# Five small constant loads issued behind the three weight blocks of the first projection, and a semaphore of its own for the rotation table

## The reference, cut to what matters

```python
proj = x @ w_in                      # 512x1024 @ 1024x1536
q, k, v = split(proj)                # 16 query heads, 4 key heads, 4 value heads
q = partial_rope(q, pos); k = partial_rope(k, pos)    # table of cos and sin: rope
...
probs = softmax(concat([scores, sink_col]))[..., :-1]  # swa_sinks
...
logits = (h2 @ w_router) + b_router                    # the router, after attention
...
f_logit = proj[..., 3 * hd_all:] + b_f                 # layer 1, forget gate: fox_b_f, last 16 columns of fox_w_in
```

## Time and profile before

| | us |
|---|---|
| median of three timed runs | 936.52 (936.02 to 937.94) |
| the profiled execution | 930.61 |
| its span, first to last instruction | 928.8 |
| around the span | 1.8 |
| PE busy | 890.1 (96%) |
| DVE busy | 537.9 (58%) |
| ACT busy | 379.0 (41%) |
| POOL busy | 119.8 (13%) |
| mean clock granted to TensorE | 0.994 of full |

### The profile page before, as it was taken

One profiled execution on the slowest core, in us unless ns is written; L12 is line 12 of the kernel. 1 busy time (PEld: TensorE's weight loads), 2 busy tenths in 40 slices (PEclk: granted clock), 3 DMA queues, 4 the chain that ended last, 5 costly groups with the idle time before them and its releaser, 6 DMA issues.

```text
span 928.8 us, 12393 instructions
## 1 busy us (share of the span) xinstructions
PE 890.1 (96%) x4460; PEld 611.9 (66%) x4460; DVE 537.9 (58%) x1110; ACT 379.0 (41%) x763; POOL 119.8 (13%) x137
## 2 busy tenths in 40 slices
PE   8899999999999999989999999999999999999985
PEld 7787777885665665537778886565786566665632
DVE  3543886457777677475323223777456866677617
ACT  3321887001555555331132224777301355555400
POOL 2000232102110000030000000232211210010021
PEclk9999999999999999999999999999999999999998
DMA  9941000018999998655053222111105999999335
GB/s 315 348 174 74 40 2 1 23 46 328 344 382 389 377 384 330 227 205 181 0 181 138 91 91 91 47 48 46 52 40 226 314 386 387 384 389 402 101 107 199
DMA packets 49701, 183.14 MB, mean 197 GB/s; under 512 B 6560, under 2 KB 6560, under 8 KB 41456
## 3 DMA queue, kind: packets, MB, share of 16 engines
q1 hardware_dynamic: 35712, 132.34, 37.8%
q0 software_dynamic: 9200, 33.33, 11.0%
q10 hardware_dynamic: 4736, 16.78, 4.7%
HBM read 159.60 MB, written 22.84 MB: 196 GB/s over the span
## 4 chain that ended last, share of the span: by engine, by line
PE 87%; DVE 5%; DMA 3%; issue 1%; SPq 1%; ACT 1%; POOL 0%; DVEq 0%; POOLq 0%; ACTq 0%
PE bank L557 17%; PE bank L558 17%; PE bank L559 17%; PE bank L843 12%; PE bank L674 4%; PE bank L655 4%; PE bank L812 3%; PE bank L699 2%; PE bank L499 2%; PE bank L718 2%; PE bank L531 2%; PE bank L760 2%; PE bank L513 1%; DMA ring<-in_swa_w_in 1%; DMA arena<-ys,pos 1%
## 5 line engine op out<-in xcount | busy, mean ns | idle before, releaser
L1406 DVE TENSOR_TENSOR gu_low<-ring,gu_high 128x1024 fp32r<-128x1024 f32 x128 | 151.2, 1222 | 53.3 <-ACT gu_high L1063 53.3
L1063 ACT CAST gu_high<-ring 128x1024 fp32r<-128x1024 f32 x128 | 127.7, 1048 | 18.5 <-DVE arena L1542 18.5
L843 PE MATMUL bank<-ring,arena 128*96 128x512 f32 x256 | 115.8, 595 | 2.9 <-DVE arena L1532 1.8
L557 PE MATMUL bank<-gu_high,rows_high 128*96 128x512 f32 x256 | 112.4, 439 | 2.5 <-DVE rows_low L1526 2.5
L558 PE MATMUL bank<-gu_low,rows_high 128*96 128x512 f32 x256 | 101.0, 395 | 0.0
L559 PE MATMUL bank<-gu_high,rows_low 128*96 128x512 f32 x256 | 100.5, 393 | 0.0
L843 PEld LDWEIGHTS bank<-ring,arena 128*96 128x96 f32 x256 | 39.7, 165 | 55.3 <-issue 54.5
L995 ACT ACTIVATE arena<-arena,nmax 128x256 f32<-128x256 f32 (+3 forms) x128 | 66.8, 523 | 20.9 <-DVE nmax L1299 10.8
L557 PE MATMUL bank<-high,x_high 128*128 128x512 f32 x160 | 64.9, 406 | 6.2 <-DVE xlow L1209 3.5
L447 POOL TENSOR_TENSOR low<-ring,high 128x512 fp32r<-128x512 f32 x32 | 40.6, 1270 | 227.7 <-ACT high L1023 227.7
L558 PE MATMUL bank<-low,x_high 128*128 128x512 f32 x160 | 63.9, 400 | 0.0
(11 more groups left out here) (227 smaller groups left out, 1499.4 us busy)
## 6 DMA issues: line engine op xcount, KB each, us to landing
ring<-in_w_gate SPq DMA_DIRECT2D x32, 1024.0 KB, 13.6
ring<-in_w_up SPq DMA_DIRECT2D x32, 1024.0 KB, 16.0
ring<-in_w_down SPq DMA_DIRECT2D x32, 1024.0 KB, 16.3
ys<-arena ACTq DMA_DIRECT2D x32, 384.0 KB, 7.6
ring<-in_fox_w_in SPq DMA_DIRECT2D x6, 2048.0 KB, 9.4
ring<-in_swa_w_in SPq DMA_DIRECT2D x2, 2048.0 KB, 13.4
ring<-in_swa_w_o SPq DMA_DIRECT2D x2, 2048.0 KB, 17.6
xd<-xres ACTq DMA_DIRECT2D x8, 512.0 KB, 2.6
```

What stands on the lines that cost most here:

```text
L557: eng.matmul(out, ah, wh, start=(c == 0), stop=False)
L843: mm = eng.matmul(bank[5 + half][0:CAP, :], hT[:, b, c, :], w[:, c, half * BLK:(half + 1) * BLK], start=(c == 0), stop=(c == FC - 1))
L1063: eng.copy(gu_high[u % 2][:, :, part, :], slot_gate_up(use)[:, :, part, :]).then_inc(S("gu_high"), 1)
L1406: eng.tensor_tensor(gu_low[use % RING][:, :, part, :], slot_gate_up(use)[:, :, part, :], gu_high[u % 2][:, :, part, :], ALU.subtract).then ...
```

## The change

The five small loads that nobody reads in the projection (`sink`, `wr`, `br`, `bf`, `wf`) are issued behind block 2. The rotation table stays where it was and gets the semaphore `rope_in`. Tiles 2 and 3 of x follow it directly. DVE waits for `rope_in` at its old place, and for the other five (`const_in`, now 80) at the start of the last group, k = 11, where it now negates the sinks. PE waits for 80 instead of 96 ahead of the router.

```diff
                     if l == 0 and j == 0:
                         load_x(1)
-                        eng.dma_start(cs[:, :, :, :], rope.rearrange("(t p) a n -> p t a n", p=P)).then_inc(S("const_in"), 16)
+                        eng.dma_start(cs[:, :, :, :], rope.rearrange("(t p) a n -> p t a n", p=P)).then_inc(S("rope_in"), 16)
+                        load_x(2)
+                        load_x(3)
+                    if l == 0 and j == IN_BLOCKS[0] - 1:
                         eng.dma_start(sink[:, :], swa_sinks[0].partition_broadcast(P)).then_inc(S("const_in"), 16)
                         eng.dma_start(wr[:, :, :], w_router.rearrange("(c p) n -> p c n", p=P)).then_inc(S("const_in"), 16)
                         eng.dma_start(br[:, :], b_router.partition_broadcast(P)).then_inc(S("const_in"), 16)
                         eng.dma_start(bf[:, :], fox_b_f.rearrange("a h -> h a")).then_inc(S("const_in"), 16)
                         eng.dma_start(wf[:, :, :], fox_w_in[0][:, 3 * D:3 * D + NH].rearrange("(c p) n -> p c n", p=P)).then_inc(S("const_in"), 16)
-                        load_x(2)
-                        load_x(3)
...
                     if t == 0:
-                        eng.wait_ge(S("const_in"), 96)
+                        eng.wait_ge(S("const_in"), 80)
...
-            eng.wait_ge(S("const_in"), 96)
-            link(eng.tensor_scalar(sink[:, :], sink[:, :], -1.0, None, ALU.mult))
+            eng.wait_ge(S("rope_in"), 16)
...
                     for k in range(GROUPS[0]):
                         j, t = k // NT, k % NT
+                        if k == GROUPS[0] - 1:
+                            eng.wait_ge(S("const_in"), 80)
+                            link(eng.tensor_scalar(sink[:, :], sink[:, :], -1.0, None, ALU.mult))
                         if k + 1 < NT:
                             x_low(k + 1)
```

## The result

| | before | changed |
|---|---|---|
| median of seven runs, us | 936.02 (932.88 to 937.94) | 928.77 (926.73 to 931.24) |
| ratio of the runs | | 0.9932, interval 0.9916 to 0.9949 |
| profiled execution, its span, us | 930.61, 928.8 | 928.77, 927.0 |

By the ratio the change is worth 6.4 us (4.8 to 7.9), not 3.9; a second measurement (experiment 12) gives 5.3 us (3.5 to 7.1). The two profiled spans differ by 1.8 us only, and why that is no measure of the change is one of the things to be learned here.

The account below looks back on a forecast made before the run. PE was taken to bound the kernel, with a 3.52 us stall at group 2 behind block 1's load. An earlier landing (2.3 us) plus the clock (1.56) gave 3.9 us, 936.5 to 932.6 us, range 931.0 to 935.0.

Parts of the forecast that it names:

- The bound: PE stands 3.52 us at group 2, since ACT waits for block 1; PE starts 2.72 us after block 1 lands.
- the landing: Block 1's load lands at 20.9 instead of 23.26, 2.3 us earlier, leaving a stall of 1.2 us at group 2.
- Rival A: PE's stall at group 2 goes wholly, block 1 landing by 19.74: gain 5.1 us, time 931.4; chance 0.12.
- the trough: DMA at 10 to 14 us: 164 instead of 398 GB/s, from small pieces and SP's hold, costing 2.35 us.
- The clock: PE's clock no longer falls in the 4.42 us behind the group 2 stall: 1.56 us come back.
- the new semaphore: DVE waits for the table alone at its old place: nothing gained, nothing lost.
- the wait at group 11: DVE's added wait for the five loads and the negation fit in 4.50 us of idle time: cost 0.
- POOL: Gets block 2 earlier and starts clearing `ys` some 2 us before 29.41: cost 0.
- SP's queue: Issue of block 1 or 2 takes several us, but a full queue holds SP, not the transfers: cost 0.
- B: The clock behind group 2's stall falls all the same, only 2.3 us won: 934.2; chance 0.15.
- C: SP's stop moves from `br` to block 1, which lands near 23, no earlier: 936.5; chance 0.07.
- D: Queue not served in order, so block 0 and groups 0 and 1 come late: 5.8 us slower, 942.4; chance 0.04.

Follow-up runs that it names:

- experiment 12: The changed kernel measured again as it is: 929.84 us, ratio 0.9943 to before.
- Experiment 1: Kernel before, loads untouched; ACT and DVE make the next block's weight pieces behind the next tile of x instead of ahead of it: 928.13 us, ratio 0.9937.
- experiment 3: Changed kernel, but only `wr` and `wf` moved behind block 2; `sink`, `br`, `bf` stay in front: 933.27 us, ratio 0.9988.
- experiment 4: Changed kernel, but only `sink`, `br`, `bf` moved behind block 2; `wr` and `wf` stay in front: 935.0 us, ratio 1.0002.
- experiment 5: Changed kernel with the load of `sink` alone back between the table and tile 2: 932.27 us in one run.
- experiment 10: Changed kernel with the load of `wr` alone back between the table and tile 2: 934.87 us in one run.
- experiment 11: Changed kernel with `sink` alone in front, the same program repeated and timed: 932.55 us, ratio 0.9976.
- experiment 9: Changed kernel plus a probe load ahead of tile 2, 128 pieces of 64 bytes from different rows of x, read by nobody: 930.01 us in one run.
- Experiment 2: Kernel before with only the change's semaphores, all loads in the old order: 933.45 us, ratio 0.9991.

## Why the prediction was wrong, point by point

*The bound was right.* The wait, its cause on ACT, the 2.72 us from landing to start: the six stalls measured later follow from it. With `wr` and `wf` gone, 22.03 + 2.7 = 24.7, and PE started at 24.72; in the other five PE started 2.69 to 2.70 us behind ACT's first piece as well. Experiment 1 shows the cause by itself.

*The step that failed is the landing.* "Sum 2.35 + 0.37 - 0.42 = 2.3 us. Block 1 lands at 23.26 - 2.3 = 20.9." It moved by 3.9 us in the profiled execution, and by 3.1 in experiment 12 (23.26 to 20.15). What the sum left out can in part be read from the trace that I had. Up to block 1's landing before, and in the changed kernel (length, clock, DMA share, GB/s):

```profile
0.00:23.26 23.26, 1.00 0.91 315
```

```profile
0.00:19.36 19.36, 1.00 0.93 345
```

23.26 us at 315 GB/s are 7.33 MB; x, block 0 and block 1 (2.1 MB each) with the table and the small loads (0.21), all that lies in the queue up to the last piece of block 1, are 6.50. So 0.8 MB from behind block 1 had passed before block 1 was whole. With the change it is 6.68 MB against 6.36, 0.3 MB. The 0.5 MB between them, at 390 GB/s, are 1.3 us. And the table, for which I kept 0.42 us, cost next to nothing (391 GB/s with it in the stretch). 2.35 + 0.37 + 1.3 is 4.0. The same reckoning on the other traces gives 0.5 MB (experiment 12) and 0.6 (probe or `bf` in front) where block 1 lands at 20.1 to 20.5, and 0.7 to 1.1 in experiments 3, 4, 5, 10 and 11, where it lands at 22.0 to 23.0. That the 16 engines were out of step, so that some were already at the next block while others still had a share of this one, is the reading that I put on these bytes; no view shows the engines one by one.

Rival A, which I gave 0.12, is what happened as to the stall. Two things in it are off. In the later profiles block 1 lands at 20.15 to 20.48, behind A's 19.74, and the stall is gone all the same, since PE came to group 2 later there (experiment 12). And the estimate of 3.9 us that stood for it was near the measured 3.9 and 3.1 by luck: it adds a price for each load by itself, but with `bf` or the probe alone in front block 1 lands within 0.3 us of experiment 12's 20.15, and with `sink` or `wr` alone 2.2 to 2.7 us behind it.

*The cause of the trough was only half right.* I put it on many small pieces and SP's hold. Experiments 5, 9 and 11 show a third: 128 pieces that read the same 64 bytes take the rate to 271 and 324 GB/s in two executions, as many pieces from different places leave it at 393. With experiment 10 they also show why halves of the change are worth so little: `sink` alone, `wr` alone, or `wr` and `wf` together are each enough to put block 1 at 22.4 to 23.0.

*The clock.* I took one fall of 1.56 us as certain, because the one profile had it behind the stall. Experiment 2 had the stall without the fall. Over many runs the kernels with the stall lose 2 to 3 us more to the clock than those without, by the first table of experiment 12, which is 0.4 to 1.4 us more than my term. The second table shows where: the fall behind the stall came in four of seven executions, and a second place, 157 to 160 us, in five of them; nine falls of 1.7 us over seven executions are 2.2 us for each. Why the stall at 22 us should bring a fall at 157 no run here shows, and with this few profiles the counts may be scatter.

*The sum.* 3.9 predicted, 6.4 and 5.3 measured; the second interval (3.5 to 7.1) takes in 3.9, the first (4.8 to 7.9) does not. 1.2 us are the stall that I left standing, about 1 us the clock; what is left is inside the intervals. By itself the landing would have given A's 931.4, still in the range. The time also lies lower because the median of before is 936.02 over seven runs and not 936.52. The range was too narrow for that: its lower end gave rival A 0.4 us of scatter, while the medians of the changed kernel alone are 928.77 and 929.84, and those of before 934.31 to 936.02.

*Right at no cost:* the new semaphore (experiment 2), the wait at group 11 (row above), POOL, and SP's queue, which was held for longer than I thought and delayed nobody. Rivals B, C and D did not happen: PE's first matmul of group 0 came at 8.89 us against 8.88, so block 0 was not disturbed by what was queued behind it.

## What to carry to other kernels

A wait for a large load costs what stands behind it in the same engine's stream; look there first, since putting independent work ahead of it gave the same 6 us as all the reordering of loads. In this queue a broadcast of one short row to all partitions was not a small load: 8 KB of it put block 1 at 22.4 to 22.8 us, nearly as late as the 128 KB of `wr` and `wf` (23.0), and with `sink` alone, with `sink`, `br` and `bf`, or with `wr` and `wf` left in front more than half of the gain was gone (ratios 0.9976, 0.9988 and 1.0002). Two single profiles whose clock fell in different places must not be subtracted: count the falls, or compare only up to the first of them.

## What the runs showed of the hardware

- 128 pieces of 64 bytes from one place: 271 and 324 GB/s over 4 us in two executions. As many from 128 places: 393 in one.
- An issue on SP can take 5 to 6 us for a load of 8 KB (5.29 and 6.16 us for `sink` and `br`) while the transfers ahead of it run at full share (1.05 from 14 to 22 us). The issue of the same `br` took 4.13 us with `wr` ahead of it and 0.57 without.
- Up to 1.1 MB of later loads had passed before a block of 2.1 MB was whole, behind a stretch of small pieces; 0.3 to 0.6 MB without `sink` or `wr` in front.
- The granted clock fell at five places of these programs (26, 157, 221 to 231, 405 to 412 and 734 us), each time behind a thin stretch of PE, in some executions and not in others; three of the falls cost 1.56, 1.68 and 1.67 us. Behind PE's stall at group 2 it fell in four profiles (stalls of 2.2 to 3.5 us) and stayed full in three (1.4, 3.0 and 3.4 us), so the length of the stall alone does not decide it.
- Granted clock and time go together from run to run: 926.7 us at 0.996, 931.2 at 0.992 for the changed kernel.
